# Gated attention output: split into halves by ScalarE and GpSimd and turned by DMA, for 15 of 16 tiles

## The chip, the cores and the metric

One core of one Trainium2 chip. The metric is the device time of one launch in microseconds; the kernel before was run three times, with a median of 1634.67 us (1633.82 to 1635.09).

## The reference

One residual block over x of 4096 rows by 1024, in float32. After an RMSNorm one input projection feeds a pooling mixer (512 wide) and a chunked attention (8 heads of 64, chunks of 64 rows, each reading itself and 8 chunks before it, with a clipped relative bias). What matters here is the end of the attention branch:

```
p = softmax(q k^T * scale + bias)              # per head
y_attn = (p v) * silu(gate)                    # 4096 x 512, this is the "gated output"
x = x + concat(y_pool, y_attn) @ w_out         # the attention half of w_out is 512 x 1024
out = rms_norm(x, final_norm_gain)
```

## The kernel before

Three phases follow each other: the norm and the values and gates of all rows; the pooling branch with its part of the output product, added to the residual in DRAM; and the attention phase (the `a_phase_...` functions), the one that is touched. Float32 matmuls are replaced by three float16 ones: each operand is split into a high half and a low half (the rest), and high*high, high*low and low*high are summed.

The attention phase goes over 16 tiles t of 256 rows (two blocks j of 128), and in each over 8 heads h. A head of a full tile takes some 6 us, a tile 48.9 us. Nothing is scheduled at run time: each of the five engines (TensorE is PE, VectorE DVE, ScalarE ACT, GpSimd POOL, SyncE SP) has its own hand-written order, and semaphores join them. Within a head PE runs scores, values of the head before, the maxima of two heads ahead, and in three places of a head (`other`, slots x = 3h + 0, 1, 2) extra work: the seven key and query products of a later tile (L1740 to L1743), and, in slots 7 to 16 of tile t, the output product of tile t-1 (`output`, L2007), 48 matmuls of 512 columns.

The gated output is `y` (128 rows, 2 blocks j, 512 columns, float32). DVE writes a head's 64 columns in `attend` (L2276 reciprocal, L2282 gating), one head late: the last head of tile t-1 in head 0 of tile t. The output product wants `y` turned, as float16 halves. Before, this goes in two rounds per tile, round 0 for columns 0 to 255 in head 0 of tile t, round 1 for columns 256 to 511 in head 1. A round is: PE turns four 128x128 float32 blocks with the identity into the PSUM bank `tra` (`branch_transposes`, L2075); ACT copies them to the high half `yT_h` (`branch_hi`, L2140); DVE makes the low half `yT_l` (`branch_lo`, L2250). The bank `tra` also takes the row maxima (`max_rows`, L1947), which therefore wait for `branch_lo`. The output product's first matmul, in head 2, waits for both rounds. The last tile (LAST, t = 15) has rounds of its own at other places.

Every second head's probabilities are turned in another way (`turn`, L1880): one DMA transpose on SP's queue turns `r16` (128 x 2560 float16, 20 blocks of 128x128) into `pT`. SP issues all loads and stores in one fixed order. For tile t it is: turn of head 1, `load_v` (L1820), `load_gate` (L1826), the two residual loads of tile t-1 (L2417), three key/query operand loads (L1809), turn of head 3, four more such loads, moves of keys and queries (L1854 to L1872), turn of head 5, loads, a store, turn of head 7, moves, the second store (L2421). On POOL a head's low halves (`p_lo` L2367, `row_lo` L2383) and a 128x1024 subtraction for the next keys or queries (`kq_lo`, L1786; its ACT half `kq_hi` is L1782) come in a fixed order too.

Of the kernel before, what the change touches and what calls it, by code (L numbers as in the profile page):

```python
# [17 lines left out]
ALU = mybir.AluOpType  # L18
SCRATCH = 4096
ACT = mybir.ActivationFunctionType  # L20
# [87 lines left out]
def build(nc, x, norm_gain, w_in, pool_w, pool_scale, rel_fwd, rel_rev, w_out, final_gain, out):  # L108
# [13 lines left out]
    with ctx:  # L122
        def sb(name, shape, dt):
            return ctx.enter_context(nc.sbuf_tensor(name, shape, dt))
# [25 lines left out]
        mx = sb("row_max", [P, 2, 2], F32)  # L150
        nm = sb("row_shift", [P, 2, 2], F32)


# [65 lines left out]
        junk2 = view(Z, 33792, (640,), BF16)  # L219
        yT_h = view(Z, 35072, (NKT, AT), F16)  # L220
        yT_l = view(Z, 37120, (NKT, AT), F16)
        r32 = view(X, 0, (2, 640), F32)
# [641 lines left out]
        def h_phase_pool(pool):  # L864
# [16 lines left out]
            def v12_lo(p):  # L881
# [16 lines left out]
            nc.gpsimd.memset(vst[:, :, :].rearrange("p e (h d) -> p e h d", d=DH + 1)[:, :, :, DH:DH + 1],  # L898
                             1.0).then_inc(H["consts"], 1)
            rstd(2)  # L900
# [574 lines left out]
        def q_phase_sp(sp):  # L1475
# [87 lines left out]
            bias_k_loaded mask_done fg_loaded wob_hi wob_lo out_mm out_done  # L1563
            rows_set shift_done rexp_done rph_done rpl_done max_mm max_done mrow_mm mrow_done st_mm bias_done exp_done ph_done pl_done
            pv_mm rc_done ya_done yt_mm yth_done ytl_done ss_done ms_done rstd_done fin_done""".split()
        A = {n: sem("a_" + n) for n in names}
        wob_loaded = [sem(f"a_wob_loaded{n}") for n in range(NKT)]
        hop3_loaded = entry_loaded
        turned = sem("a_turned")

        moved_k = [sem(f"a_moved_k{s}") for s in range(2)]
# [12 lines left out]
        KSCALE, QSCALE = 1 / WS, 1 / (WS * math.sqrt(DH))  # L1584
        YSCALE = YS * 0.5
        LAST = ATILES - 1
# [31 lines left out]
        def by_rows(h):  # L1618

            return h % 2 == 1  # L1620
# [54 lines left out]
        def round_at(t, h):  # L1675

            if t > 0 and h < 2:
                return t - 1, h
            return {HALF + 1: (t, 0), HEADS - 1: (t, 1)}.get(h) if t == LAST else None

        def round_kts(t, r):
# [106 lines left out]
        def attention_masks(pool):  # L1788
            for r in range(RING // 2):
                k_rows = kl[DH:P, r, 0, :, :].rearrange("p h (b c k) -> p (h b) c k", c=2, k=CHUNK)  # L1790
                nc.gpsimd.memset(k_rows[:, :, 0, :], -MASK).then_inc(A["mask_rows"], 1)
                nc.gpsimd.memset(k_rows[:, :, 1, :], 0.0).then_inc(A["mask_rows"], 1)
            q_rows = qm[DH:P, 0, :, :].rearrange("p h (j c k) -> p (h j) c k", c=2, k=CHUNK)
            nc.gpsimd.memset(q_rows[:, :, 0, :], 0.0).then_inc(A["mask_rows"], 1)
            nc.gpsimd.memset(q_rows[:, :, 1, :], MASK).then_inc(A["mask_rows"], 1)
            pool.wait_ge(A["mask_rows"], 2 * (RING // 2) + 2)
            nc.gpsimd.memset(r16[:, :, :, :], 0.0).then_inc(A["rows_set"], 1)

# [75 lines left out]
        def turn(sp, t, h):  # L1874
            head = HEADS * t + h
            if head == 1:
                sp.wait_ge(A["rows_set"], 1)
            sp.wait_ge(A["rpl_done"], row_count(t, h, 1) + 1)
            at_least(sp, A["pv_mm"], head - 1)
            sp.dma_start_transpose(pT[:, :, :, :, :].rearrange("p j a i n -> p (j a i) n"),  # L1880
                                   r16[:, :, :, :].rearrange("p j a n -> p (j a n)")).then_inc(turned, 16)
# [55 lines left out]
        def max_rows(pe, t, h):  # L1937

            pe.wait_ge(A["max_done"], 2 * (HEADS * t + h + 1))
            if t > 0 or h > 0:  # L1940
                pe.wait_ge(A["mrow_done"], HALF * t + h // 2)
            for back in (h - 3, h - 2):
                if back >= 0 and round_at(t, back):
                    of, r = round_at(t, back)
                    pe.wait_ge(A["ytl_done"], 2 * of + r + 1)
            for j in range(2):
                mm = nc.tensor.matmul(tra[:, j * P:(j + 1) * P], m16[:, h // 2 % 2, j:j + 1].to_broadcast([P, P]),  # L1947
                                      ident16[:, :], start=True, stop=True)
            mm.then_inc(A["mrow_mm"], 1)
# [37 lines left out]
        def a_phase_pe(pe):  # L1987
            def output(t, i, first, end):

                j, n2 = i // 2, i % 2  # L1990
                if first == 0:
                    pe.wait_ge(A["ytl_done"], 2 * t + (1 if t == LAST else 2))
                    if t == 0 and i == 0:
                        pe.wait_ge(A["wob_lo"], NKT)
                    if t == LAST and i >= 2:
                        pe.wait_ge(A["max_done"], 2 * HEADS * ATILES)
                    else:
                        at_least(pe, A["out_done"], 4 * t + i - 1)
                    if i < 2 and t < LAST:
                        pe.wait_ge(A["kq_u"], 5 * min(2 * t + 6, 2 * ATILES) - 1 + i)  # L2000
                elif t == LAST:
                    pe.wait_ge(A["ytl_done"], 2 * t + first // 3)
                for m in range(first, end):
                    kt, p = m // 3, m % 3
                    yh = (yT_l if p == 2 else yT_h)[:, kt, j * P:(j + 1) * P]
                    w = (wob_l if p == 1 else wob_h)[:, kt, n2 * 512:(n2 + 1) * 512]
                    mm = nc.tensor.matmul(out_bank(t, i), yh, w, start=(m == 0), stop=(m == 11))  # L2007
                if end == 12:
                    mm.then_inc(A["out_mm"], 1)
# [56 lines left out]
            def branch_transposes(t, r, rows):  # L2066
# [4 lines left out]
                if t == LAST and r > 0:  # L2071
                    pe.wait_ge(A["ytl_done"], 2 * t + r)
                for q in range(2 * (end - first)):
# [62 lines left out]
        def a_phase_act(act):  # L2136
            def branch_hi(t, r):
                act.wait_ge(A["yt_mm"], 2 * t + r + 1)
                first, end = round_kts(t, r)
                nc.scalar.activation(yT_h[:, first:end, :],  # L2140
                                     tra[:, 0:(end - first) * AT].rearrange("p (k n) -> p k n", k=end - first),
                                     ACT.Copy, scale=YSCALE).then_inc(A["yth_done"], 1)

# [52 lines left out]
            def wob_hi(n):  # L2196
                act.wait_ge(wob_loaded[n], 16)
                nc.scalar.activation(wob_h[:, n, :], res[:, n % 2, :], ACT.Copy, scale=WS).then_inc(A["wob_hi"], 1)
# [10 lines left out]
            def head(t, h):  # L2209
# [17 lines left out]
                if round_at(t, h):  # L2227
                    branch_hi(*round_at(t, h))
                other(t, h, 2)
                for of, j in squares_at(t, h):  # L2230
# [15 lines left out]
        def a_phase_dve(dve):  # L2246
            def branch_lo(t, r):
                dve.wait_ge(A["yth_done"], 2 * t + r + 1)
                first, end = round_kts(t, r)
                nc.vector.scalar_tensor_tensor(  # L2250
                    out=yT_l[:, first:end, :], in0=tra[:, 0:(end - first) * AT].rearrange("p (k n) -> p k n", k=end - first),
                    scalar=YSCALE, in1=yT_h[:, first:end, :],
                    op0=ALU.mult, op1=ALU.subtract).then_inc(A["ytl_done"], 1)

# [14 lines left out]
            def attend(t, h):  # L2269
# [8 lines left out]
                if h % HALF == 0:  # L2278
                    dve.wait_ge(gate_loaded[h // HALF], 16 * (t + 1))
                    at_least(dve, A["yt_mm"], 2 * (t - 1) + 1 + h // HALF)  # L2280
                for j in range(2):
# [79 lines left out]
        def a_phase_pool(pool):  # L2361
# [18 lines left out]
            def row_lo(t, h, j):  # L2380
# [3 lines left out]
                                        ALU.subtract).then_inc(A["rpl_done"], 1)  # L2384

            row_lo(0, 1, 0)
            for t in range(ATILES):
                for h in range(HEADS):
# [17 lines left out]
                    if split_at(t, h):  # L2406
                        kq_lo(pool, split_at(t, h))
                    if by_rows(h) and t < 2:
                        row_lo(t2, h2, 0)
# [3 lines left out]
        def a_phase_sp(sp):  # L2413
# [5 lines left out]
            def store(t, j):  # L2419
                sp.wait_ge(A["fin_done"], 2 * t + j + 1)  # L2420
                sp.dma_start(out_blk[2 * t + j], res[:, j, :]).then_inc(out_stored[j], 16)  # L2421

            def load_wob(n):
                at_least(sp, A["wob_lo"], n - 1)
                sp.dma_start(res[:, n % 2, :], wout_v[NKT + n]).then_inc(wob_loaded[n], 16)

            for t in range(ATILES):
# [11 lines left out]
                else:  # L2439
# [3 lines left out]
                    if t == 1:  # L2443
                        sp.wait_ge(A["wob_lo"], NKT)
                    for j in range(2):
                        load_residual(t - 1, j)
# [23 lines left out]
                move_k(sp, t + 1, 1)  # L2470
                move_q(sp, t + 1, 1)
                if t > 0:
                    store(t - 1, 1)
# [62 lines left out]
```

## Time and profile before

| what | value |
|---|---|
| median of three runs | 1634.67 us |
| the profiled execution | 1639.75 us, span 1638.0 us |
| PE busy | 1580.3 us, 96% of the span |
| DVE, ACT, POOL busy | 63%, 50%, 40% of the span |
| mean granted TensorE clock | 0.988 of full speed |
| DMA, queue of SP | 61.8% of 16 engines' span |

All rows are from the one profiled execution. A tile's rows repeat from tile to tile: tile 3, from 986.8 us on, stands for them. In a timeline row the columns are start, duration, engine, line, operation, output<-input, count, and in brackets how long the engine was idle before and what ended that.

### The profile page before, as it was taken

To read this page: it belongs to the slowest core of one execution; us is meant where nothing else is said; L and a number is where in the kernel's file an instruction comes from. 1 tells how busy PE (TensorE), PEld (TensorE's weight loads), DVE (VectorE), ACT (ScalarE), POOL (GpSimd) and SP (SyncE) were. 2 spreads that over 40 slices of the span, in tenths; PEclk is the share of its full clock that TensorE was granted. 3 is DMA by queue.
4 is the path that set the end of the run, shared out by engine and by line. 5 is a ranking of instruction groups with operands and counts; after the bars stand their busy time and mean duration, and the time that the engine had idled before them with its cause. 6 is when DMAs were issued, how large, how long until landed. Compare 5 with 4: busy or idle time off the path is not lost.

```text
span 1638.0 us, 42689 instructions
## 1 busy us (share of the span) xinstructions
PE 1580.3 (96%) x17344; PEld 1181.3 (72%) x17344; DVE 1037.9 (63%) x2134; ACT 826.2 (50%) x1541; POOL 662.9 (40%) x667
## 2 busy tenths in 40 slices
PE   7999999999999999999988999999999999999976
PEld 3455455458677777767767888899888899888853
DVE  7977867747565576556435666666666666666654
ACT  6655545522121111111125777767777777677763
POOL 2543433311101121111313655655655665656653
PEclk9999999999999999999998999999999999999978
DMA  6656566473524524542777877877777877778663
GB/s 245 218 193 219 188 212 221 181 258 147 207 75 169 206 96 150 181 167 79 222 220 185 208 196 199 198 187 192 171 193 196 201 192 184 172 190 197 158 170 84
DMA packets 306459, 299.99 MB, mean 183 GB/s; under 512 B 179384, under 2 KB 239816, under 8 KB 304216
## 3 DMA queue, kind: packets, MB, share of 16 engines
q1 hardware_dynamic: 305736, 296.60, 61.8%
q8 instruction: 138, 2.26, 0.6%
q0 software_dynamic: 528, 0.66, 0.2%
q14 instruction: 57, 0.47, 0.1%
HBM read 150.87 MB, written 83.54 MB: 143 GB/s over the span
## 4 chain that ended last, share of the span: by engine, by line
PE 68%; DMA 4%; POOL 2%; ACT 2%; SPq 2%; DVE 1%; issue 1%; DVEq 0%; ACTq 0%; POOLq 0%
PE bank L1154 10%; PE bank L2007 8%; PE bank L1130 6%; PE bank L1133 6%; PE bank L1132 6%; PE bank L1740 5%; PE bank L1742 5%; PE bank L1743 5%; DMA stages<-rows 4%; PE bank L1930 3%; PE bank L2061 2%; PE bank L2063 2%; PE bank L2062 2%; PE bank L2027 2%; PE bank L1933 2%
## 5 line engine op out<-in xcount | busy, mean ns | idle before, releaser
L1740 PE MATMUL bank<-middle,weights 128*128 128x128 f16 x1792 | 311.2, 220 | 2.3 <-ACT middle L1756 1.3
L1742 PE MATMUL bank<-middle,weights 128*128 128x128 f16 x1792 | 310.9, 220 | 0.0
L1743 PE MATMUL bank<-middle,weights 128*128 128x128 f16 x1792 | 310.8, 220 | 0.0
L2383 POOL TENSOR_TENSOR rows<-rows 128x640 f16<-128x640 f32 (+4 forms) x128 | 172.8, 1350 | 274.6 <-ACT rows L2184 274.6
L1130 PE MATMUL bank<-middle 128*128 128x256 f16 x784 | 213.7, 273 | 0.5 <-DVE stages L1270 0.5
L1133 PE MATMUL bank<-middle 128*128 128x256 f16 x784 | 213.7, 273 | 0.0
L1132 PE MATMUL bank<-middle 128*128 128x256 f16 x784 | 213.7, 273 | 0.0
L2007 PE MATMUL bank<-entry,stages 128*128 128x512 f16 x768 | 190.6, 386 | 5.3 <-DVE stages L2250 5.3
L1740 PEld LDWEIGHTS bank<-middle,weights 128*128 128x128 f16 x1792 | 176.0, 98 | 3.7 <-issue 2.8
L1742 PEld LDWEIGHTS bank<-middle,weights 128*128 128x128 f16 x1792 | 176.0, 98 | 0.4
L1743 PEld LDWEIGHTS bank<-middle,weights 128*128 128x128 f16 x1792 | 175.8, 98 | 0.0
L1154 PE MATMUL bank<-entry,stages 128*128 128x512 f16 x768 | 169.6, 379 | 0.5 <-DVE middle L1773 0.5
L1436 POOL TENSOR_TENSOR stages<-stages 128x512 f16<-128x512 f32 x32 | 38.2, 1194 | 307.1 <-ACT stages L1215 307.1
L2367 POOL TENSOR_TENSOR stages<-stages 128x512 f16<-128x512 f32 (+2 forms) x124 | 151.8, 1239 | 13.4 <-ACT stages L2171 13.4
L341 PE MATMUL bank<-weights,middle 128*128 128x512 f16 x392 | 148.6, 379 | 3.8 <-DVE stages L706 1.7
L344 PE MATMUL bank<-weights,middle 128*128 128x512 f16 x392 | 148.6, 379 | 0.0
L343 PE MATMUL bank<-weights,middle 128*128 128x512 f16 x392 | 148.6, 379 | 0.0
L1930 PE MATMUL bank<-middle 128*128 128x128 f16 (+1 forms) x848 | 136.2, 244 | 9.5 <-DVE row_max L1971 6.1
L1154 PEld LDWEIGHTS bank<-entry,stages 128*128 128x128 f16 x768 | 74.9, 98 | 86.0 <-DVE middle L1773 0.6
L2061 PE MATMUL bank<-middle,stages 128*128 128x65 f16 x1200 | 124.0, 194 | 12.7 <-POOL stages L2367 7.2
L1773 DVE SCALAR_TENSOR_TENSOR middle<-bank,middle 128x256 f32<-128x256 f32 x160 | 67.6, 423 | 97.3 <-PE bank L1743 81.8
L2061 PEld LDWEIGHTS bank<-middle,stages 128*128 128x128 f16 x1200 | 111.3, 98 | 22.1 <-POOL stages L2367 8.6
(169 smaller groups left out, 3956.0 us busy)
## 6 DMA issues: line engine op xcount, KB each, us to landing
entry<-in_x SPq DMA_DIRECT2D x64, 512.0 KB, 3.8
h_ops<-middle SPq DMA_DIRECT2D x16, 1792.0 KB, 6.1
middle<-h_ops SPq DMA_DIRECT2D x112, 256.0 KB, 5.4
middle<-h_ops SPq DMA_DIRECT2D x49, 512.0 KB, 8.0
residual<-entry SPq DMA_DIRECT2D x32, 512.0 KB, 3.0
middle<-middle SPq DMA_DIRECT2D x128, 128.0 KB, 3.2
out<-entry SPq DMA_DIRECT2D x31, 512.0 KB, 2.9
entry<-residual SPq DMA_DIRECT2D x30, 512.0 KB, 5.6
```

Of the source, the lines that this page charges most:

```text
L1130: nc.tensor.matmul(bank, wh, hop[:, :, s, 0, kt, :], start=(kt == 0 and s < 4), stop=False, skip_group_check=True)
L1132: nc.tensor.matmul(bank, wh, hop[:, :, s, 1, kt, :], start=False, stop=False, skip_group_check=True)
L1133: mm = nc.tensor.matmul(bank, wl, hop[:, :, s, 0, kt, :], start=False, stop=(kt == 3), skip_group_check=True)
L1154: mm = nc.tensor.matmul(op_bank(n, n2), part, w[:, kt, n2 * 512:(n2 + 1) * 512], start=(kt == 0 and w is wot_h and part is yh), stop=(kt = ...
L1740: nc.tensor.matmul(dst, wh, hop3[:, o, 0, kt, :], start=(kt == 0 and s < 2 and pair == 0), stop=False, skip_group_check=True)
L1742: nc.tensor.matmul(dst, wh, hop3[:, o, 1, kt, :], start=False, stop=False, skip_group_check=True)
L1743: mm = nc.tensor.matmul(dst, wl, hop3[:, o, 0, kt, :], start=False, stop=(kt == 3), skip_group_check=True)
L1930: mm = nc.tensor.matmul(wide[:, c:c + n * P], q, keys(ks, every, h, ring(t, i), n), start=True, stop=not by_rows(h))
L2007: mm = nc.tensor.matmul(out_bank(t, i), yh, w, start=(m == 0), stop=(m == 11))
L2061: nc.tensor.matmul(acc, ph, vh, start=(i == blocks[0]), stop=False)
L2367: nc.gpsimd.tensor_tensor(p_l[:, c + a:c + b], p32[g][:, a:b], p_h[:, c + a:c + b], ALU.subtract).then_inc(A["pl_done"], 1)
L2383: nc.gpsimd.tensor_tensor(r16[:, j, 1, c:640], r32[:, j, c:640], r16[:, j, 0, c:640], ALU.subtract).then_inc(A["rpl_done"], 1)
```

## The change

For tiles 0 to 14 the two PE rounds go. A new function on ACT (`turn_hi`) copies half of `y` to a float16 buffer `y16`, POOL (`turn_lo`) subtracts for the low half, and a DMA transpose on SP (`turn_y`, 128 x 1024 float16, 8 blocks) writes both halves turned to `yT`. The first half (part 0) of tile t goes in its own head 6, the second in head 0 of tile t+1; on SP the first stands after the last moves of tile t and before the second store, the second after `load_gate` and before the residual loads. The output product waits for the DMAs in place of `branch_lo`. The scale that `branch_hi` applied goes into the ones of the value tensor. Tile 15 keeps its rounds. The scratch for software DMAs is halved to make room for `y16`.

```diff
-SCRATCH = 4096
+SCRATCH = 2048
+        y16 = sb("branch_halves", [P, 2, 2, 2 * P], F16)
-        yT_h = view(Z, 35072, (NKT, AT), F16)
-        yT_l = view(Z, 37120, (NKT, AT), F16)
+        yT = view(Z, 35072, (2, 2, 2, AT), F16)
 (ones of the values)
-                             1.0).then_inc(H["consts"], 1)
+                             2 / YS).then_inc(H["consts"], 1)
 (round_at)
-            if t > 0 and h < 2:
-                return t - 1, h
             return {HALF + 1: (t, 0), HEADS - 1: (t, 1)}.get(h) if t == LAST else None
+        def turn_at(t, h):
+            if h == 0 and t > 0:
+                return t - 1, 1
+            return (t, 0) if h == HALF + 2 and t < LAST else None
 (PE, output)
-                    pe.wait_ge(A["ytl_done"], 2 * t + (1 if t == LAST else 2))
+                    if t == LAST:
+                        pe.wait_ge(A["ytl_done"], 1)
+                    else:
+                        pe.wait_ge(y_turned, 32 * (t + 1))
 (ACT; called in head after branch_hi, that is after the head's exponentials and kq_hi)
+            def turn_hi(t, r):
+                act.wait_ge(A["ya_done"], 2 * (HEADS * t + HALF * (r + 1)))
+                at_least(act, y_turned, 16 * (2 * t + r))
+                nc.scalar.activation(y16[:, 0, :, :].rearrange("p k (j n) -> p k j n", j=2),
+                                     y[:, :, 2 * r * P:(2 * r + 2) * P].rearrange("p j (k n) -> p k j n", k=2),
+                                     ACT.Copy).then_inc(A["yth16_done"], 1)
 (DVE, attend of heads 0 and 4)
-                    at_least(dve, A["yt_mm"], 2 * (t - 1) + 1 + h // HALF)
+                    at_least(dve, A["ytl16_done"], 2 * (t - 1) + 1 + h // HALF)
 (POOL; called in head after kq_lo)
+            def turn_lo(t, r):
+                pool.wait_ge(A["yth16_done"], 2 * t + r + 1)
+                nc.gpsimd.tensor_tensor(y16[:, 1, :, :]..., y[...], y16[:, 0, :, :]...,
+                                        ALU.subtract).then_inc(A["ytl16_done"], 1)
 (SP)
+            def turn_y(t, r):
+                sp.wait_ge(A["ytl16_done"], 2 * t + r + 1)
+                at_least(sp, A["out_mm"], 4 * t)
+                sp.dma_start_transpose(yT[:, r, :, :, :].rearrange("p a k (j n) -> p (a k j) n", j=2),
+                                       y16[:, :, :, :].rearrange("p a k n -> p (a k n)")).then_inc(y_turned, 16)
                     load_gate(sp, t, 1)
                     if t == 1:
                         sp.wait_ge(A["wob_lo"], NKT)
+                    turn_y(t - 1, 1)
                     for j in range(2):
                         load_residual(t - 1, j)
...
                 move_q(sp, t + 1, 1)
+                turn_y(t, 0)
                 if t > 0:
                     store(t - 1, 1)
```

## Rows read from the trace of the kernel before

**Rows 1.** The page, its head.
```profile
span 1638.0 us, 42689 instructions
```

**Rows 2.** Windows, tile 3: length; busy (count) PE, PEld, DVE, ACT, POOL; clock; DMA; GB/s.
```profile
993.10:1041.90 48.80, 48.80 (x786) 42.46 (x784) 31.86 (x78) 35.33 (x65) 29.48 (x26) 1.00 0.76 190
```

**Rows 3.** Waits of PE, 940 to 1550 us: who for whom, total, times, longest.
```profile
PE bank L2061 <- POOL stages L2367: 1.9, 3, 1.2
```

**Rows 4.** Waits of PE, 1550 us to the end.
```profile
PE bank L2007 <- DVE stages L2250: 5.3, 2, 2.8
...
PE bank L1947 <- DVE stages L2250: 1.4, 1, 1.4
```

**Rows 5.** Timeline of PE: a round of tile 2 and the output product's start.
```profile
986.84 0.60 PE L2075 MATMUL bank<-ident,middle 128*128 128x128 f32 x4
987.28 0.22 PE L1740 MATMUL bank<-middle,weights 128*128 128x128 f16 x1
...
997.95 0.60 PE L2007 MATMUL bank<-entry,stages 128*128 128x512 f16 x2
```

**Rows 6.** Timeline of DVE: last gating of tile 2, low half, first residual sum.
```profile
986.97 0.47 DVE L2282 SCALAR_TENSOR_TENSOR middle<-bank,rc,middle 128x64 f32<-128x64 f32 x2
...
988.92 0.69 DVE L2250 SCALAR_TENSOR_TENSOR stages<-bank,stages 128x512 f16<-128x512 f32 x1 [0.74 <-ACT stages L2140]
...
1001.94 0.69 DVE L2294 SCALAR_TENSOR_TENSOR entry<-bank,entry 128x512 f32<-128x512 f32 x1 [0.58 <-PE bank L2007]
```

**Rows 7.** Timeline of ACT, heads 6 to 0 around the tile's edge.
```profile
976.96 0.39 ACT L1756 ACTIVATE middle<-bank 128x256 f32<-128x256 f32 x1 [1.42 <-PE bank L1743]
...
987.37 1.04 ACT L1782 ACTIVATE middle<-middle 128x1024 f16<-128x1024 f32 x1
988.31 0.58 ACT L2140 ACTIVATE stages<-bank 128x512 f16<-128x512 f32 x1
```

**Rows 8.** Timeline of POOL, heads 6 to 0 around the tile's edge.
```profile
981.20 1.40 POOL L2383 TENSOR_TENSOR rows<-rows 128x640 f16<-128x640 f32 x1 [2.66 <-ACT rows L2184]
...
984.79 1.40 POOL L2383 TENSOR_TENSOR rows<-rows 128x640 f16<-128x640 f32 x1 [1.14 <-ACT rows L2184]
...
987.54 1.16 POOL L2367 TENSOR_TENSOR stages<-stages 128x512 f16<-128x512 f32 x1 [0.23 <-ACT stages L2171]
988.65 2.13 POOL L1786 TENSOR_TENSOR middle<-middle 128x1024 f16<-128x1024 f32 x1
```

**Rows 9.** Timeline of SP around the tile's edge; duration is that of the issue.
```profile
985.30 0.58 SPq L2421 DMA_DIRECT2D out<-entry  x1
986.80 3.08 SPq L1880 DMA_TRANSPOSE stages<-rows  x1
...
992.05 0.94 SPq L2417 DMA_DIRECT2D entry<-residual  x2
```

**Rows 10.** Lines L1880 and L2417 from 940 to 1550 us: issues and landings.
```profile
L1880 SPq DMA_TRANSPOSE stages<-rows x50: 2990/3129/3849, 937.9 to 1539.9; - x50
...
DMA to landing us min/median/max: 4.8/5.0/7.0
...
L2417 SPq DMA_DIRECT2D entry<-residual x26: 429/448/468, 944.5 to 1533.3; - x26
...
DMA to landing us min/median/max: 3.6/5.7/6.7
```

**Rows 11.** The page's DMA issues: the smallest frequent copy within the chip.
```profile
middle<-middle SPq DMA_DIRECT2D x128, 64.0 KB, 2.5
```

**Rows 12.** Tile 15: SP, ACT, and line L1880's landings from 1570 us on.
```profile
1579.45 1.18 SPq L2417 DMA_DIRECT2D entry<-residual  x2
...
1581.02 0.74 ACT L2184 ACTIVATE rows<-rows 128x640 f16<-128x640 f32 x1 [2.45 <-DMA stages<-rows]
...
DMA to landing us min/median/max: 6.5/6.6/6.7
```

More of the change, by code:

```diff
@@ L1563, in build @@
             bias_k_loaded mask_done fg_loaded wob_hi wob_lo out_mm out_done
-            rows_set shift_done rexp_done rph_done rpl_done max_mm max_done mrow_mm mrow_done st_mm bias_done exp_done ph_done pl_done
-            pv_mm rc_done ya_done yt_mm yth_done ytl_done ss_done ms_done rstd_done fin_done""".split()
+            shift_done rexp_done rph_done rpl_done max_mm max_done mrow_mm mrow_done st_mm bias_done exp_done ph_done pl_done
+            pv_mm rc_done ya_done yt_mm yth_done ytl_done yth16_done ytl16_done ss_done ms_done rstd_done fin_done""".split()
         A = {n: sem("a_" + n) for n in names}
-        wob_loaded = [sem(f"a_wob_loaded{n}") for n in range(NKT)]
+        wob_loaded = [sem(f"a_wob_loaded{n}") for n in range(2)]
         hop3_loaded = entry_loaded
         turned = sem("a_turned")
+        y_turned = sem("a_y_turned")
         moved_k = [sem(f"a_moved_k{s}") for s in range(2)]
@@ L1584, in build @@
         KSCALE, QSCALE = 1 / WS, 1 / (WS * math.sqrt(DH))
-        YSCALE = YS * 0.5
         LAST = ATILES - 1
@@ L1675, in round_at, with turned_part @@
         def round_at(t, h):
-            if t > 0 and h < 2:
-                return t - 1, h
             return {HALF + 1: (t, 0), HEADS - 1: (t, 1)}.get(h) if t == LAST else None
+        def turn_at(t, h):
+            if h == 0 and t > 0:
+                return t - 1, 1
+            return (t, 0) if h == HALF + 2 and t < LAST else None
+        def turned_part(part, kts):
+            first = kts.start
+            return yT[:, first // 2, part, first % 2:first % 2 + kts.stop - first, :]
         def round_kts(t, r):
@@ L1796, in attention_masks @@
             pool.wait_ge(A["mask_rows"], 2 * (RING // 2) + 2)
-            nc.gpsimd.memset(r16[:, :, :, :], 0.0).then_inc(A["rows_set"], 1)
+            nc.gpsimd.memset(r16[:, :, :, :], 0.0).then_inc(A["mask_rows"], 1)
         def key_ones(pool):
@@ L1876, in turn @@
             if head == 1:
-                sp.wait_ge(A["rows_set"], 1)
+                sp.wait_ge(A["mask_rows"], 2 * (RING // 2) + 3)
             sp.wait_ge(A["rpl_done"], row_count(t, h, 1) + 1)
@@ L1943, in max_rows @@
                 if back >= 0 and round_at(t, back):
-                    of, r = round_at(t, back)
-                    pe.wait_ge(A["ytl_done"], 2 * of + r + 1)
+                    _, r = round_at(t, back)
+                    pe.wait_ge(A["ytl_done"], r + 1)
             for j in range(2):
@@ L2001, in output @@
                 elif t == LAST:
-                    pe.wait_ge(A["ytl_done"], 2 * t + first // 3)
+                    pe.wait_ge(A["ytl_done"], first // 3)
                 for m in range(first, end):
                     kt, p = m // 3, m % 3
-                    yh = (yT_l if p == 2 else yT_h)[:, kt, j * P:(j + 1) * P]
+                    yh = yT[:, kt // 2, 1 if p == 2 else 0, kt % 2, j * P:(j + 1) * P]
                     w = (wob_l if p == 1 else wob_h)[:, kt, n2 * 512:(n2 + 1) * 512]
@@ L2071, in branch_transposes @@
                 if t == LAST and r > 0:
-                    pe.wait_ge(A["ytl_done"], 2 * t + r)
+                    pe.wait_ge(A["ytl_done"], r)
                 for q in range(2 * (end - first)):
@@ L2137, in branch_hi @@
             def branch_hi(t, r):
-                act.wait_ge(A["yt_mm"], 2 * t + r + 1)
+                act.wait_ge(A["yt_mm"], r + 1)
                 first, end = round_kts(t, r)
-                nc.scalar.activation(yT_h[:, first:end, :],
+                if r == 0:
+                    act.wait_ge(A["out_mm"], 4 * t)
+                nc.scalar.activation(turned_part(0, slice(first, end)),
                                      tra[:, 0:(end - first) * AT].rearrange("p (k n) -> p k n", k=end - first),
-                                     ACT.Copy, scale=YSCALE).then_inc(A["yth_done"], 1)
+                                     ACT.Copy).then_inc(A["yth_done"], 1)
+            def turn_hi(t, r):
[4 more added lines that the diff above has]
+                                     ACT.Copy).then_inc(A["yth16_done"], 1)
             def max_row(t, h):
@@ L2196, in wob_hi @@
             def wob_hi(n):
-                act.wait_ge(wob_loaded[n], 16)
+                act.wait_ge(wob_loaded[n % 2], 16 * (n // 2 + 1))
                 nc.scalar.activation(wob_h[:, n, :], res[:, n % 2, :], ACT.Copy, scale=WS).then_inc(A["wob_hi"], 1)
@@ L2228, in head @@
                     branch_hi(*round_at(t, h))
+                if turn_at(t, h):
+                    turn_hi(*turn_at(t, h))
                 other(t, h, 2)
@@ L2247, in branch_lo @@
             def branch_lo(t, r):
-                dve.wait_ge(A["yth_done"], 2 * t + r + 1)
+                dve.wait_ge(A["yth_done"], r + 1)
                 first, end = round_kts(t, r)
[L2250 to L2253, printed above, removed]
+                nc.vector.tensor_tensor(
+                    turned_part(1, slice(first, end)),
+                    tra[:, 0:(end - first) * AT].rearrange("p (k n) -> p k n", k=end - first),
+                    turned_part(0, slice(first, end)), ALU.subtract).then_inc(A["ytl_done"], 1)
             def add_bias(t, h):
@@ L2384, in row_lo @@
                                         ALU.subtract).then_inc(A["rpl_done"], 1)
+            def turn_lo(t, r):
+                pool.wait_ge(A["yth16_done"], 2 * t + r + 1)
+                nc.gpsimd.tensor_tensor(y16[:, 1, :, :].rearrange("p k (j n) -> p k j n", j=2),
+                                        y[:, :, 2 * r * P:(2 * r + 2) * P].rearrange("p j (k n) -> p k j n", k=2),
+                                        y16[:, 0, :, :].rearrange("p k (j n) -> p k j n", j=2),
+                                        ALU.subtract).then_inc(A["ytl16_done"], 1)
             row_lo(0, 1, 0)
@@ L2407, in a_phase_pool @@
                         kq_lo(pool, split_at(t, h))
+                    if turn_at(t, h):
+                        turn_lo(*turn_at(t, h))
                     if by_rows(h) and t < 2:
@@ L2421, in store @@
                 sp.dma_start(out_blk[2 * t + j], res[:, j, :]).then_inc(out_stored[j], 16)
+            def turn_y(t, r):
[3 more added lines that the diff above has]
+                                       y16[:, :, :, :].rearrange("p a k n -> p (a k n)")).then_inc(y_turned, 16)
             def load_wob(n):
                 at_least(sp, A["wob_lo"], n - 1)
-                sp.dma_start(res[:, n % 2, :], wout_v[NKT + n]).then_inc(wob_loaded[n], 16)
+                sp.dma_start(res[:, n % 2, :], wout_v[NKT + n]).then_inc(wob_loaded[n % 2], 16)
             for t in range(ATILES):
```

## The prediction

> **What bounds the kernel now.** I read the busy shares first, tile by tile: in tile 3, which stands for tiles 2 to 13, PE is busy for 48.80 of 48.80 us at the full clock, while ACT, DVE and POOL have 13 to 19 us to spare [rows 2]. Then PE's waits: between 940 and 1550 us they come to 1.9 us, in three places, all for POOL's low halves [rows 3]. So in the middle of the attention phase, and that is where the change lies, each tenth of a microsecond taken from PE ends the tile a tenth sooner, and nothing that other engines are spared counts, until a new wait appears. Tile 15 is another stage: there PE waits, 5.3 us for the low halves of the rounds alone [rows 4], and less PE work buys little.
>
> **What is removed.** One round is four transposes. The first starts at 986.84 us and the next product's first matmul at 987.28, so a round holds PE for 0.44 us, although the group's row says 0.60, since a matmul's end overlaps its successor [rows 5]. Two rounds make 0.88 us a tile. Tiles 0 to 14 lose them. With them go two ACT copies (0.58 us each [rows 7]) and two DVE subtractions (0.69 us each, one with 0.74 us of waiting for ACT ahead of it [rows 6]); both engines have room, so I count these at nothing. The row maxima no longer wait for the low half in the same bank; in the middle PE never waited for that, in tile 15 once, 1.4 us [rows 4].
>
> **What is added, first half.** ACT's copy in head 6 falls where ACT idles 1.42 us before its next operation, POOL's subtraction where POOL idles 2.66 us [rows 7, 8]. A 512-column subtraction takes POOL 1.16 us [rows 8], the ACT copy about the 0.58 us of the one it replaces. Neither is on a path. SP's turn stands before the second store, which is issued at 985.30; the next turn of probabilities starts at 986.80, after POOL's row half, which ended at 984.79 + 1.40 = 986.19: 0.61 us is the time from POOL's end to SP's issue [rows 8, 9]. So SP idles 0.9 us there. I put the issue of a turn of 8 blocks at 1.6 us: 0.6 us as for a plain copy, and 8/20 of the other 2.5 us that the 20-block one takes [rows 9]. The probabilities' turn is thus some 0.7 us late at worst; at 986.80 + 0.7 + 5.0 = 992.5 it lands, and PE takes it up only behind the output product's first part, after 997 us [rows 5, 10]. Nothing.
>
> **What is added, second half.** This is the one that decides. Its path, in tile 3's times: the last gating ends at 987.44 [rows 6]. ACT is in its 1024-column copy until 988.41 [rows 7], then makes the high half, until 989.0. Behind it nothing new waits, as the old copy stood in the same place. POOL is in its 1024-column subtraction until 988.65 + 2.13 = 990.78 and only then does the low half, until 991.94 [rows 8]. SP has issued the gate load by 992.05, where today the residual loads go out [rows 9]; with the 0.61 us from POOL to SP the turn is issued at 992.55. PE wants the result at the output product's first matmul, now at 997.95 and, both rounds gone, at 997.07 [rows 5]. So the transfer has 4.5 us.
>
> How long it takes no row shows, since no turn of 8 blocks is in this trace. From below, the 64 KB copies land in 2.5 us [rows 11]; from above, a turn of 20 blocks lands in 5.0 us in the median, 4.8 at best and 7.0 at worst, and the residual load that holds the same place in the queue today lands in 5.7, with twice the bytes (512 KB against 256) and behind the same loads [rows 10]. The estimate in proportion is 2.5 + 8/20 x 2.5 = 3.5 us, landing at 996.05: 1 us ahead of PE. The upper bounds 5.0 and 5.7 give 997.55 and 998.25, a wait of 0.5 to 1.2 us. I take 996.5, nearer the estimate because half the bytes are gone, so that PE waits in a few tiles only, 0.1 us in the mean. If the cover went altogether, the wait would be paid by PE in full.
>
> The Trainium skill speaks against the exchange (VectorE: DVE Perf Modes, The three transpose paths, and its Rules for kernel authors): a 128x128 turn is 390 ns on TensorE and 1309 ns by DMA, and TensorE is to be used where PSUM will do. By its price eight blocks would take 8 x 1309 ns = 10.5 us, land near 1003 and cost PE 6 us a tile, some 67 us in all. The trace does not agree with that price within one DMA: 20 blocks land in 5.0 us, a quarter of a microsecond each [rows 10].
>
> **What the turn pushes back.** The residual loads go out some 2.1 us later (0.5 of waiting, 1.6 of issue) and, the turn's own transfer ahead of them, land about 999 to 1001; DVE adds the first at 1001.94 - 0.88 = 1001.06 [rows 6, 10]. That is covered, by little for the first. The operand loads behind them serve products three heads later. The turn of head 3 finds a longer queue and may land up to 2 us late; ACT then waits before its next row copy, POOL and PE after it. The three PE waits in the middle are of that kind, 0.6 us each in the mean [rows 3], and I add 0.4 us for the whole phase.
>
> **Sum.** Tiles 2 to 14 turn over 13 times: 13 x 0.88 = 11.4 us gained. Back go 13 x 0.1 = 1.3 and 0.4 us. In tile 1 the heads are shorter, fewer key blocks being there, so the transfer has less time than its rounds gave: nothing. In tile 15 the output product starts after a wait for ACT, which itself stands for the probabilities' turn until 1581.02 [rows 4, 12]; the new path passes by that, but its turn is issued about 1579.45 and the four turns there land only 6.5 to 6.7 us after issue [rows 12]. By proportion it lands near 1583, when the product starts today, by the full time near 1586. I count it at nothing, with -1.5 and +2.5 us as ends. Net -9.7 us. Against the profiled execution, 1639.75 us (span 1638.0 [rows 1]), that is 1630.0; the runs' median 1634.67 stands 5.08 us below this execution, so the predicted median is 1625.0 us. The smaller software scratch serves one load ahead of this phase; it costs nothing that I can place.
>
> **Rivals.**
>
> *Fully hidden, and the tail gains* (0.13): no wait at all, 14 x 0.88 = 12.3 us and 1.5 us in tile 15. 1634.67 - 13.8 = 1620.9. For it: 1 us of margin by the proportional estimate. Against: the tail's slow landings.
>
> *Half eaten* (0.15): the turn lands as a full one, 5.0 us after issue, at 997.55; PE waits 0.5 us a tile. 13 x 0.4 = 5.2 gained, less 0.4: about 1629.9; with the queue's 5.7 the wait is 1.2, more than the round, and the time 1634.67 + 13 x 0.3 = 1638.6. For it: issue and landing of a small DMA have a fixed share that I can't see apart. Against: a 64 KB copy lands in 2.5 us.
>
> *Slower, the queue decides* (0.07): the second turn stands behind the probabilities' turn and three loads, and lands as the slow turns do, 6.6 us after issue, at 999.15. PE then stands at the output product 2.1 us in every tile against 0.88 gained: 13 x 1.2 = 15.6 us, 1650. It decides from 997.95 on: a landing later than 5.4 us after issue loses. For it: all four turns of tile 15 take that long [rows 12] and one of the middle takes 7.0 [rows 10]. Against: the median in the middle is 5.0 for two and a half times the blocks.
>
> *Slower, each block a transfer of its own* (0.01): eight blocks one after the other, each as long as a 64 KB copy, 8 x 2.5 = 20 us against the 4.5 there are: PE would wait 15.5 us a tile, 13 x 14.6 = 190 us, some 1825. Against: 20 blocks land in 5.0 us [rows 10, 11]. The price per block that the Trainium skill states (VectorE: DVE Perf Modes, The three transpose paths) points this way, at half that cost.
>
> *It does not do what it says* (0.02): the rounds go but PE was held by something that fills the same time; about 1634. Rows 2 and 3 exclude nearly all of it.
>
> **Chances.** The forecast has 0.62 and spans 1622.5 to 1628.5 by itself. A measurement of this kernel tells a change from none at about 0.2%, 3.3 us: faster is below 1631.4. Forecast, first rival and half of the second: faster 0.82. The rest of the second and the last: within 0.2%, 0.09. Slower 0.09. The range of 8 in 10 reaches from 1620 to 1633, with the full-tail case and most of the half-eaten one.
>
> **What would show it.** In the changed profile the tile should take 48.0 us in place of 48.9, line L2075's count fall from 128 to 8, POOL gain 30 operations of about 1.2 us. The new turns should number 30 and land in 3 to 4.5 us. A row of PE waiting at the output product for the DMA of `y` is the test: absent or under 2 us in all before 1550 us, the forecast is right; 6 us or more, a rival is. If ACT waits for the first half's turn before it overwrites `y16`, I have missed a wait; POOL's 1.8 us between 989.0 and 990.78 would cover that much. The prediction is wrong if the tile stays at 48.9 us.

## The result and the profile after

The changed kernel takes 1642.46 us (median of 5, 1639.92 to 1643.91) against 1634.67 of the kernel before on the same chip: ratio 1.0046, 95% interval 1.0029 to 1.0062. Forecast were 1625.0 us, 1620 to 1633; it came out 7.8 us slower than before. The profiled execution alone would mislead: its span equals that of before [rows 1]. The stretch from the start of tile 15 took 60.0 us in the first profile of before and 54.9 in a second one, so single spans are off by some 5 us there; the medians and the tiles in the middle are what counts. A tile is counted here from the reciprocal of its head 0 to that of the next tile.

The page of the kernel after, head and busy times:

```profile
span 1638.1 us, 42508 instructions
...
PE 1567.2 (96%) x17224; PEld 1166.6 (71%) x17224; DVE 1016.9 (62%) x2104; ACT 826.7 (50%) x1541; POOL 698.5 (43%) x697
```

PE has lost 120 instructions and 13.1 us of work, as the forecast has it. Yet the tile is no shorter: the median of tiles 2 to 13 is 49.0 us against 48.9. Together these twelve tiles take 588.8 us before and 592.5 after; PE's work in them falls by 7.5 us and its idle time rises from 1.9 to 13.1 (windows as in [rows 2], before, then after):

```profile
944.20:1533.00 588.80, 586.88 (x9411) 509.95 (x9409) 376.45 (x936) 425.21 (x769) 355.39 (x312) 1.00 0.77 190
```

```profile
946.20:1538.70 592.50, 579.40 (x9315) 499.66 (x9316) 357.33 (x914) 425.58 (x770) 382.99 (x336) 1.00 0.86 200
```

Where the gain went shows in PE's waits from 940 to 1550 us, against [rows 3], and in ACT's waits for turns in the same stretch, first of after, then of the second profile of before:

```profile
PE bank L2072 <- POOL stages L2389: 6.0, 6, 1.7
PE bank L2018 <- DMA stages<-branch_halves: 4.3, 4, 1.7
PE bank L1748 <- ACT middle L1764: 2.1, 3, 1.3
PE bank L1938 <- DVE row_max L1979: 0.2, 1, 0.2
...
ACT rows L2204 <- DMA stages<-rows: 55.1, 36, 3.1
...
ACT branch_halves L2160 <- DMA stages<-branch_halves: 1.4, 3, 0.8
```

```profile
PE bank L2061 <- POOL stages L2367: 1.8, 3, 1.1
...
ACT rows L2184 <- DMA stages<-rows: 26.0, 25, 2.6
```

PE now waits 12.6 us where it waited 1.8 to 1.9: a third for the turned y, two thirds for POOL and ACT. ACT's own wait for the probabilities' turns has doubled, and POOL works on what ACT gives it. These turns are the ones whose row has changed, against [rows 10] (line L1888 of after, 940 to 1550 us; then line L2457 of the new turns and line L2452 of the two stores):

```profile
L1888 SPq DMA_TRANSPOSE stages<-rows x50: 3000/3644/4904, 941.5 to 1545.4; - x50
...
DMA to landing us min/median/max: 4.9/5.9/7.9
...
L2457 SPq DMA_TRANSPOSE stages<-branch_halves x26: 1261/1264/3074, 939.6 to 1539.4; - x26
...
DMA to landing us min/median/max: 3.1/3.8/5.2
...
L2452 SPq DMA_DIRECT2D out<-entry x25: 338/582/1436, 940.9 to 1531.8; - x25
...
DMA to landing us min/median/max: 2.8/3.6/5.4
```

The new turns themselves are about as cheap as estimated: 1.26 us of issue (1.6 estimated), 3.1 us to landing at best and 3.8 in the median (3.5 estimated). What they do to their neighbours shows in SP's timeline at the edge of tile 4, beside [rows 9], with ACT's and PE's rows of the same moments (behind them the store and the turn of head 1 at the same edge before):

```profile
1037.53 1.26 SPq L2457 DMA_TRANSPOSE stages<-branch_halves  x1
1038.83 0.58 SPq L2452 DMA_DIRECT2D out<-entry  x1
1039.52 4.90 SPq L1888 DMA_TRANSPOSE stages<-rows  x1
1044.46 1.25 SPq L1828 DMA_DIRECT2D middle<-values  x2
1045.75 0.60 SPq L1834 DMA_DIRECT2D middle<-gates  x1
1046.45 1.26 SPq L2457 DMA_TRANSPOSE stages<-branch_halves  x1
...
1046.48 0.74 ACT L2204 ACTIVATE rows<-rows 128x640 f16<-128x640 f32 x1 [0.93 <-DMA stages<-rows]
1047.24 0.39 ACT L1764 ACTIVATE middle<-bank 128x256 f32<-128x256 f32 x1
...
1047.68 0.23 PE L1748 MATMUL bank<-middle,weights 128*128 128x128 f16 x1 [0.25 <-ACT middle L1764]
...
1051.60 0.39 PE L2018 MATMUL bank<-entry,stages 128*128 128x512 f16 x1 [1.67 <-DMA stages<-branch_halves]
```

```profile
1033.41 0.58 SPq L2421 DMA_DIRECT2D out<-entry  x1
1035.67 3.50 SPq L1880 DMA_TRANSPOSE stages<-rows  x1
```

The first half's turn and the store go out back to back, and the probabilities' turn right behind: 0.7 us after the store, where it was 2.3 before. Its issue takes 4.90 us instead of 3.50, it lands at 1046.4, 6.9 us after issue instead of 5.2, and ACT, which must not overwrite `r16` before, stands 0.93 us; its next copy makes PE wait 0.25. The loads and the second half's turn can only go out behind that long issue, and PE waits 1.67 us for y.

### The profile page after: what moved, and what is told of

Read it like the earlier page. It is cut to its first block, busy times and chain, and to the rows that moved or that the text cites. A ratio compares the mean times of both kernels' runs of the same rounds, so it can differ in the third digit from the quotient of the medians.

```text
span 1638.1 us, 42508 instructions
## 1 busy us (share of the span) xinstructions
PE 1567.2 (96%) x17224; PEld 1166.6 (71%) x17224; DVE 1016.9 (62%) x2104; ACT 826.7 (50%) x1541; POOL 698.5 (43%) x697
## 4 chain that ended last, share of the span: by engine, by line
PE 56%; DMA 10%; SPq 5%; POOL 4%; ACT 3%; issue 3%; DVE 1%; ACTq 0%; DVEq 0%; POOLq 0%
PE bank L1154 10%; DMA stages<-rows 7%; PE bank L1130 6%; PE bank L1133 6%; PE bank L1132 6%; PE bank L2018 6%; PE bank L1748 4%; PE bank L1751 3%; PE bank L1750 3%; DMA stages<-branch_halves 2%; POOL stages L2389 2%; PE bank L1938 2%; SPq L1888 2%; PE bank L2072 2%; PE bank L2074 1%
## 5 line engine op out<-in xcount | busy, mean ns | idle before, releaser
L1938 PE MATMUL bank<-middle 128*128 128x128 f16 (+1 forms) x848 | 135.9, 244 | 10.3 <-DVE row_max L1979 5.8
```

Of the source, the lines that this page charges most:

```text
L1938: mm = nc.tensor.matmul(wide[:, c:c + n * P], q, keys(ks, every, h, ring(t, i), n), start=True, stop=not by_rows(h))
```

## The experiments

Theory Q: the turns of y fill SP's queue ahead of the probabilities' turns of heads 1 and 3; these land late, ACT waits for them, and through POOL that comes to PE. Rival W: PE's wait for y at the output product is the whole loss. Rival H: the added work on ACT and POOL is. Turn 1 and turn 3 are the turns of the probabilities of heads 1 and 3. Ratios are to the kernel before, run again beside each group of runs (medians 1634.2 to 1634.7 us), with their 95% intervals.

**No turn of y.** The DMA and its waits are left out:

```diff
-                        pe.wait_ge(y_turned, 32 * (t + 1))
...
+                    if t < LAST:
+                        yh = (wob_l if p == 2 else wob_h)[:, kt, j * P:(j + 1) * P]
...
-                    turn_y(t - 1, 1)
...
-                turn_y(t, 0)
```

> The changed kernel with its 30 DMA turns of y left out (the output product of tiles 0 to 14 reads a weight tile in place of the turned y, so that part of the output is not the reference's); ACT's and POOL's halves stay. Theory Q (the turns load SP's queue, the probabilities' turns land late, ACT and POOL pass that on to PE): all of the loss goes, 1622 to 1626 us. Rival W (only PE's wait for the turned y at the output product costs): the same, 1622 to 1626. Rival H (the halves on ACT and POOL are what delays): still 1638 to 1643.

1624.93 us, 0.9938 (0.9920 to 0.9956). H falls: all of ACT's and POOL's new work is in it, and so are the smaller scratch, the moved scale and the semaphores that the change merges. Q and W both forecast this. Head 0's reciprocals come 47.97 us apart over tiles 3 and 4 (the 17 rows below, one a head, span two tiles), 0.89 less than before; over tiles 2 to 13 the median is 48.15. ACT waits 32.6 us for the probabilities' turns, against 26.0 before. The reciprocal's line, 990 to 1090 us:

```profile
L2298 DVE RECIPROCAL rc<-bank x17: 169/170/171, 991.7 to 1087.6; 128x2 f32<-128x2 f32 x17
```

The waits of the same run, 940 to 1550 us:

```profile
PE bank L2072 <- POOL stages L2389: 3.1, 4, 1.0
...
ACT rows L2204 <- DMA stages<-rows: 32.6, 30, 2.5
```

**Turns kept, nobody on PE waits for them.**

```diff
-                        pe.wait_ge(y_turned, 32 * (t + 1))
...
+                    if t < LAST:
+                        yh = (wob_l if p == 2 else wob_h)[:, kt, j * P:(j + 1) * P]
...
+                    act.wait_ge(y_turned, 32 * LAST)
```

> The changed kernel with all DMA turns of y kept, but the output product of tiles 0 to 14 reads a weight tile and waits for no turn (that part of the output is not the reference's). Theory Q: most of the loss stays, since the queue is as full as before: 1633 to 1640 us, with PE waiting for POOL's low halves and ACT's copies. Rival W: the loss goes, 1624 to 1629. Rival H: 1636 to 1643.

1638.0 us, 1.0020 (1.0007 to 1.0033). W falls as the main cause: of the 17.5 us between the two runs without and with everything (1624.9 and 1642.5), 13.1 come from the turns in the queue alone and about 4.5 from PE's own wait for y (each median is good to some 2 us). The profiles show part of the 4.5 in tile 1, 46.8 us here and 48.7 in the change. In tiles 2 to 13 they show none of it: 595.2 us here, 592.5 in the change; one wait takes the other's place there. Turn 1 lands 6.2 us and turn 3 6.9 us after issue in the median of tiles 2 to 13, against 5.15 and 4.9 before. PE's time goes into waits for POOL's low halves, behind ACT's waits:

```profile
PE bank L2072 <- POOL stages L2390: 12.4, 13, 1.7
PE bank L1748 <- ACT middle L1764: 1.9, 2, 1.4
...
ACT rows L2205 <- DMA stages<-rows: 63.5, 35, 3.9
```

**One half alone.** The other half goes by the PE round of before; the semaphore counts are changed to match.

```diff
 (first half only)
+            if t > 0 and h == 1:
+                return t - 1, 1          # round_at
-                    turn_y(t - 1, 1)
 (second half only)
+            if t > 0 and h == 0:
+                return t - 1, 0          # round_at
-                turn_y(t, 0)
```

> Only the first half of y goes by ACT, POOL and DMA; the second goes by the PE round in head 1 as in the kernel before. Theory Q: the turn still stands ahead of the second store and the probabilities' turn, so little is gained: 1631 to 1637 us. Rival W: the first half lands long before PE wants it, so half of the PE gain comes, 14 x 0.44 = 6 us: 1627 to 1630. Rival H: 1634 to 1638.

> Only the second half of y goes by ACT, POOL and DMA; the first goes by the PE round in head 0 as in the kernel before. Theory Q: nothing new stands ahead of the probabilities' turn of head 1, so the value and gate loads and the y turn go out earlier and land about 0.7 us earlier than in the changed kernel; 1630 to 1636 us. Rival W: the wait at the output product stays, half of the PE gain only: 1636 to 1641. Rival H: 1634 to 1638.

1632.04 us, 0.9981 (0.9969 to 0.9993), and 1634.62, 0.9997 (0.9985 to 1.0009). Medians over tiles 2 to 13: with the first half only, turn 1 lands 6.5 us after issue (5.15 before) and turn 3 about as before (5.1 against 4.9); with the second only, turn 1 5.4 and turn 3 5.8. Each half delays the turn that stands behind it. The first time is in Q's range alone; the second is in Q's and in H's. Alone each half costs less than it gains or as much; together they lose.

**Plain copies in place of the turns,** the same 256 KB, unread:

```diff
-                sp.dma_start_transpose(yT[:, r, :, :, :].rearrange("p a k (j n) -> p (a k j) n", j=2),
-                                       y16[:, :, :, :].rearrange("p a k n -> p (a k n)")).then_inc(y_turned, 16)
+                sp.dma_start(yT[:, r, :, :, :].rearrange("p a k n -> p (a k n)"),
+                             y16[:, :, :, :].rearrange("p a k n -> p (a k n)")).then_inc(y_turned, 16)
```

> As the run with unread turns, but each of the 30 DMA turns of y is a plain copy of the same 256 KB to the same place (the output product of tiles 0 to 14 reads a weight tile, so that part of the output is not the reference's). Theory Q1 (the packets of 256 bytes of the turn hold the 16 DMA engines): 2 KB rows take the engines a shorter time, the probabilities' turns land within 0.4 us of the kernel before, and the time falls towards 1628. Rival Q2 (any 256 KB put at these two places delays what stands behind): 1635 to 1639, turns 1 and 3 about 1 us late.

1632.76 us, 0.9982 (0.9969 to 0.9995): between the two, 7.8 us above the run without any turn and 5.2 below that with unread turns, and between the ranges of Q1 and Q2. Turn 1 lands 5.7 us and turn 3 6.5 us after issue. So the same 256 KB cost as plain copies too, and as turns some two thirds more by the medians. How much of the difference is the issue (0.5 us a copy, 1.26 a turn) and how much the transfer was not tried.

**Moving the queue's entries.** First half one head earlier, its turn ahead of the turn of head 7; then also the first three operand loads behind the turn of head 5; then also y ahead of the value and gate loads.

```diff
-            return (t, 0) if h == HALF + 2 and t < LAST else None
+            return (t, 0) if h == HALF + 1 and t < LAST else None
...
+                turn_y(t, 0)
                 turn(sp, t, 7)
...
-                turn_y(t, 0)
```

> The changed kernel with the first half made one head earlier (head 5) and its DMA turn issued between the first store and the turn of head 7, ahead of the moves. Theory Q (place in the queue decides): turn 1 lands as before (5.2 us after issue, from 6.4), the second half of y 0.7 us earlier, and the time falls by 4 to 8 us to 1634 to 1638. Rival W (landing of the second half decides, by its own path): 1638 to 1642.

> As the run before, and the first three operand loads go out behind the turn of head 5 instead of ahead of the turn of head 3. Theory Q: turns 1 and 3 both land as in the kernel before, what is left is a wait at the output product in a few tiles: 1625 to 1630 us, faster than both kernels. Rival W: 1634 to 1640.

> As the run before, and the second half of y is turned ahead of the value and gate loads instead of behind them. If the wait at the output product is what is left, it goes: the second half lands by 9 us after the last gating, 1623 to 1627 us. If the place behind turn 1 in the queue matters little, the same as the run before within 2 us.

1638.75 us, 1.0022 (1.0008 to 1.0037): 3.7 better than the change, but in W's range and not in Q's. Turn 1 lands in 5.2 us again and the second half of y 0.7 us earlier, as Q has it; turn 3, which I had not counted, still lands in 6.4, and PE still waits 10.2 us for POOL, all of it ahead of the gating of head 6. In the profiles most of the gain lies in tile 1 (46.7 us, 48.7 in the change); tiles 2 to 13 take 591.8 us, 592.5 in the change. So a turn 1 on time is not enough by itself. The other two were misses of mine: 1707.92 (1.0445, 1.0425 to 1.0465) and 1710.82 us (1.0468, 1.0446 to 1.0489). I had counted the operands' first use one head too late. The waits of PE of the first of the two, 940 to 1550 us:

```profile
PE bank L1748 <- DMA middle<-h_ops: 44.9, 11, 4.9
```

Their times say nothing on Q or W.

**Order alone.** The second store ahead of the moves; in the second and third run also one operand load instead of three ahead of turn 3, and two behind turn 5, so that as many as before stand ahead of turn 5; in the third also y ahead of the value and gate loads.

```diff
+                if t > 0:
+                    store(t - 1, 1)
                 move_k(sp, t + 1, 1)
                 move_q(sp, t + 1, 1)
                 turn_y(t, 0)
-                if t > 0:
-                    store(t - 1, 1)
 (second and third run)
+                    load_hop3(sp, t + 2, 0)
+                    turn(sp, t, 3)
+                    for s in range(1, 5):
+                        load_hop3(sp, t + 2, s)
...
+                    for s in (5, 6):
+                        load_hop3(sp, t + 2, s)
```

> As the run with the first half only, and the second store issued ahead of the moves instead of behind the turn of y. Theory Q (the store behind the y turn is what the turn of head 1 stands behind): turn 1 lands 5.2 us after issue again (6.5 in the run before it), PE's waits for POOL before head 6 fall by half, and the whole gain of 14 x 0.44 us comes: 1627 to 1630 us. Rival (ACT's and POOL's half in head 6, or the y turn's own packets, delay head 0): still 1631 to 1634.

> The changed kernel with both halves by DMA, the second store ahead of the moves, one operand load instead of three ahead of the turn of head 3, and two of the seven moved behind the turn of head 5, so that the number ahead of the turn of head 5 stays. Theory Q: turns 1 and 3 land within 0.3 us of the kernel before, ACT's waits for them fall from 55 to about 30 us, and the time is 1625 to 1630 us, faster than both kernels. Rival (the packets themselves, wherever they stand, slow the turns): 1633 to 1640.

> As the run before, and the second half's turn ahead of the value and gate loads. It takes off what wait is left at the output product (2 to 4 us in all by theory Q): 1623 to 1628 us. If the y turn then waits on SP for POOL and the loads behind it push turn 3 back, no faster than the run before.

With the first half only: 1628.58 us, 0.9967 (0.9958 to 0.9976), faster than both kernels and in Q's range; turn 1 lands in 5.5 us (6.5 without the move). PE's waits for POOL fell less than forecast, from 4.2 us to 3.5 between 940 and 1550 us. With both halves: 1631.18 us, 0.9982 (0.9970 to 0.9994), 11.3 us less than the change by order alone, also a little faster than before, and 1.2 us over Q's range. Turn 1 lands in 5.6 us and turn 3 in 5.2 (6.4 and 6.1 in the change), not quite as in before, and ACT waits less; PE still waits a little for y (line L1888, then the waits, 940 to 1550 us):

```profile
L1888 SPq DMA_TRANSPOSE stages<-rows x51: 2974/3163/4047, 941.9 to 1548.4; - x51
...
DMA to landing us min/median/max: 4.8/5.2/6.8
```

```profile
PE bank L2072 <- POOL stages L2389: 3.3, 4, 1.5
PE bank L2018 <- DMA stages<-branch_halves: 2.4, 5, 0.9
...
ACT rows L2204 <- DMA stages<-rows: 35.1, 30, 3.0
```

With y ahead of the loads PE no longer waits for y in this stretch, yet the time is 1633.56 us, 0.9998 (0.9982 to 1.0014), no better than the run before it, whose interval overlaps: the loads, pushed back, now stand nearer ahead of turn 3, which lands in 6.8 us, and PE waits for POOL:

```profile
PE bank L2072 <- POOL stages L2389: 9.9, 10, 1.7
PE bank L1748 <- ACT middle L1764: 0.6, 1, 0.6
```

PE's 2.4 us for y are gone, and its waits for POOL grew from 3.3 to 9.9 us: the wait that was removed came back, larger, while turn 3 landed 1.6 us later. That is the clearest case for Q, with one reserve: ACT's wait for the first half's turn, before it overwrites `y16`, grew too, from 3.5 to 8.2 us, and what that adds was not taken apart.

**The kernel before again.**

> The kernel before, unchanged, for a second profile: tiles 2 to 13 at 48.9 us again; the stretch after the start of tile 15, 60.0 us in the first profile, may come out near 55 as in the other runs, which would show that this stretch varies from execution to execution by about 5 us whatever the kernel.

1635.8 us, one run. Tiles 2 to 13 are 48.9 us, to a tenth, but for four of 49.1 to 50.1; the stretch from the start of tile 15 takes 54.9 us, as the expectation had it.

## Why the prediction was wrong

- **PE's gain** held: 0.88 us a tile forecast, 0.89 measured where nothing waits.
- **ACT's and POOL's halves** held: 0.61 and 1.16 us. The run without turns has them and takes 1624.9 us, the forecast's own time; without the 1.3 and 0.4 us that it adds for the turns the forecast would be 1623.3, within that run's interval. They are not quite free: PE's waits for POOL are 3.1 us there, 1.9 before.
- **The turn's price** held for the first half and not for the second: 3.5 us to landing estimated, 3.1 and 4.4 in the medians of tiles 2 to 13.
- **The first half, "Nothing", failed.** The prediction looked for the harm in the issue of the probabilities' turn, "some 0.7 us late at worst", kept its landing at 5.0 us behind that, and asked only when PE takes it up. The issue is not late at all: it starts 0.04 us after the reciprocal of the last head in the median, before and after. PE's values release it last and not POOL, so the 0.61 us from POOL to SP were misread too. What changed is the landing, 6.4 us after issue instead of 5.15 (tiles 2 to 13): with the new turn ahead of it the store goes out 1.1 us before turn 1 and no longer 2.5 (medians), and ACT waits for that landing before it may refill `r16`.
- **"I add 0.4 us for the whole phase" was the term that was mis-sized.** It named the right chain, turn of head 3, ACT's row copy, POOL, PE, and priced it by the three waits that before shows [rows 3]. That row showed how often the slack ran out, not how much there was: in before ACT already waited 25 times for turns, 26 us in all. With one microsecond more on turn 1 and two on turn 3, PE waited 12.4 us for POOL with nobody waiting for y. The run with unread turns prices the whole step at 13.1 us.
- **The second half.** Forecast to land 9.7 us after the reciprocal ahead of the last gating starts (996.5 in tile 3's times), it landed 10.7 after it in the median (y of tiles 1 to 12). PE's need, where it had waited for nothing, came at 10.3, as the prediction has it. SP issued the turn 0.3 us later than forecast, since turn 1's issue takes 3.9 us in the median rather than 3.2, and it then took 4.4 us to land, not 3.95. That is 4.3 us of waits in the middle, against 1.3.
- **The signs that it named** point the same way. PE waited 6.3 us for y before 1550 us, over the 6 that were to show a rival, and the tile stayed at 49.0 us. ACT does wait for the first half's turn before it overwrites `y16`, 1.4 us in the middle. That is not the main cause: with unread turns it is 0.3 us, and the 13.1 us are lost all the same.
- **Tile 1, "nothing", failed.** It takes 48.7 us, 45.5 and 46.3 in the two profiles of before: PE waits 2.0 us for y there, and behind that wait the granted clock falls to half, the lower of its two levels, for 3.4 us (PE's wait, 890 to 940 us, then windows of after):

```profile
PE bank L2018 <- DMA stages<-branch_halves: 2.0, 1, 2.0
...
900.00:904.60 4.60, 2.62 (x35) 2.05 (x33) 1.55 (x5) 4.44 (x10) 3.00 (x5) 1.00 1.14 242
904.60:908.00 3.40, 3.40 (x30) 2.11 (x29) 1.25 (x5) 0.54 (x1) 2.92 (x2) 0.50 1.01 378
```

The reordered run with both halves has the same: 2.4 us of waiting for y, 3.4 us at half clock, a tile of 49.4 us. Where PE waits 0.8 us or not at all for y there (the first half one head earlier, y ahead of the loads in the reordered queue, unread turns), the clock stays up in tile 1 and it takes 46.6 to 46.8 us.

- **Tile 15, "nothing",** stays open: PE waits 2.7 us for y there, but the stretch from its start takes 55.6 us, between the 54.9 and 60.0 of before.
- **The rivals.** "Slower, the queue decides" had the right resource and the wrong victim: it priced a late y, and what was late above all was another transfer in the same queue.
- **The price per block** that the Trainium skill states (VectorE: DVE Perf Modes, The three transpose paths), 1309 ns for a 128x128 block by DMA, does not add up block by block here. Eight times that figure would be 10.5 us, an estimate; eight blocks of one DMA landed in 3.1 to 5.2 us.

Not settled: why the two halves together lose more than the sum of each alone. In every tile turns 1, 3 and 5 follow one another, so delays could add up along them, but that is argued and no run takes it apart; what share of tile 1's loss is the clock was not tried either.

## What to carry to other kernels

When work moves from a full engine to a queue, price the entries that stand behind the new one, not only its own path: for each, ask who waits for its landing, the engine that may not overwrite its source included, and how much that one already waits. A short list of waits on the bounding engine says that slack exists now, not how much; the waits of the engine one step upstream give a first hint (here ACT's 26 us for turns, before anything was added). They are no measure of it: with ACT's wait at 46 us PE waited 10.2 us for POOL in one run, at 55 us 6.0 in the change. Order in the queue can be worth as much as the change: here 11 us.

## What the runs showed that was not expected

A transfer's price at a fixed place in the queue depends on its kind beyond its own bytes: 30 copies of 256 KB cost 7.8 us, the same 30 as turns 13.1. The issue of a DMA turn was longer where other entries went out right ahead of it. The same instruction took 2.97 to 4.90 us in the change; turn 1's took 3.9 us in the median there, 3.2 before and 3.2 in the reordered run with both halves. Every entry of SP behind it goes out after that: at the edge of tile 4 the issue ended at 1044.42 us and the next load went out at 1044.46.
